# One more weight sum of a feed-forward block made by an adding transfer, its two source blocks loaded in the other order

## The reference

```python
h = rms_norm(x, ffn_norm_g[layer])
x = x + (jax.nn.silu(h @ w_ffn_gate[layer]) * (h @ w_ffn_up[layer])) @ w_ffn_down[layer]
return rms_norm(x, final_norm_g)
```

## Time and profile before

| | |
|---|---|
| median of 3 runs | 381.22 us (380.93 to 381.58) |
| the profiled execution's own time | 381.97 us |
| its span in the trace | 379.8 us |
| TensorE busy | 370.3 us, 97% |
| VectorE busy | 300.0 us, 79% |
| ScalarE busy | 218.1 us, 57% |
| transfers issued by SyncE (q1) | 70.03 MB, 52.9% of 16 engines' span |
| transfers issued by GpSimd (q0) | 3.15 MB, 4.9% of 16 engines' span |
| granted TensorE clock, mean | 0.995 of full |

### The profile page before, as it was taken

One profiled execution on the slowest core, in us unless ns is written; L12 is line 12 of the kernel. 1 busy time (PEld: TensorE's weight loads), 2 busy tenths in 40 slices (PEclk: granted clock), 3 DMA queues, 4 the chain that ended last, 5 costly groups with the idle time before them and its releaser, 6 DMA issues. The chain is left out here.

```text
span 379.8 us, 4716 instructions
## 1 busy us (share of the span) xinstructions
PE 370.3 (97%) x1859; PEld 311.6 (82%) x1859; DVE 300.0 (79%) x354; ACT 218.1 (57%) x253; POOL 39.7 (10%) x40
## 2 busy tenths in 40 slices
PE   7999999999999999999999999999999999999993
PEld 6998888788888888888888888888888888888782
DVE  3899986986366576289768849999999999999625
ACT  4758688675195541445356536864692692687205
POOL 2699020000000040000100000100100100000002
PEclk9999999999999999999999999999999999999998
DMA  7889165947427277166636920795796499361002
GB/s 283 266 267 298 30 200 193 333 138 253 186 62 271 112 286 267 55 221 210 247 98 209 348 107 9 189 360 220 167 344 265 122 300 352 112 220 59 0 2 110
DMA packets 40765, 73.76 MB, mean 194 GB/s; under 512 B 2300, under 2 KB 14632, under 8 KB 40744
## 3 DMA queue, kind: packets, MB, share of 16 engines
q1 hardware_dynamic: 38944, 70.03, 52.9%
q0 software_dynamic: 1584, 3.15, 4.9%
q10 hardware_dynamic: 216, 0.28, 0.2%
HBM read 72.41 MB, written 1.05 MB: 193 GB/s over the span
## 5 line engine op out<-in xcount | busy, mean ns | idle before, releaser
L976 DVE TENSOR_TENSOR w_lo<-w_raw,w_hi 128x2048 fp32r<-128x2048 f32 x33 | 75.0, 2294 | 15.0 <-ACT w_hi L619 15.0
L859 ACT ACTIVATE w_hi<-w_raw 128x2048 fp32r<-128x2048 f32 x33 | 62.8, 1914 | 24.6 <-DVE w_raw L1337 24.6
L619 ACT ACTIVATE w_hi<-w_raw 128x2048 fp32r<-128x2048 f32 x33 | 62.5, 1916 | 22.7 <-DMA w_raw<-in_w_in 10.3
L1357 DVE TENSOR_TENSOR w_lo<-w_raw,w_hi 128x2048 fp32r<-128x2048 f32 x33 | 74.6, 2285 | 0.2 <-ACT w_hi L859 0.2
L1488 PE MATMUL pp<-w_hi,hT 128*128 128x512 f32 x128 | 50.5, 395 | 0.0
L1490 PE MATMUL pp<-w_lo,hT 128*128 128x512 f32 x128 | 49.9, 390 | 0.0
L1489 PE MATMUL pp<-w_hi,hT 128*128 128x512 f32 x128 | 49.8, 389 | 0.0
L1488 PE MATMUL pp<-w_hi,yT_hi 128*128 128x512 f32 (+1 forms) x104 | 40.5, 390 | 0.0
L1490 PE MATMUL pp<-w_lo,yT_hi 128*128 128x512 f32 (+1 forms) x104 | 40.3, 388 | 0.0
L1489 PE MATMUL pp<-w_hi,yT_lo 128*128 128x512 f32 (+1 forms) x104 | 40.2, 387 | 0.0
L1488 PEld LDWEIGHTS pp<-w_hi,hT 128*128 128x128 f32 x128 | 24.0, 188 | 5.5 <-issue 0.7
(11 more groups left out here) (302 smaller groups left out, 696.1 us busy)
## 6 DMA issues: line engine op xcount, KB each, us to landing
w_raw<-in_w_in SPq DMA_DIRECT2D x21, 1024.0 KB, 5.3
w_raw<-in_w_ffn_gate SPq DMA_DIRECT2D x11, 1024.0 KB, 8.5
w_raw<-in_w_ffn_up SPq DMA_DIRECT2D x11, 1024.0 KB, 7.9
w_raw<-in_w_ffn_down SPq DMA_DIRECT2D x11, 1024.0 KB, 8.0
w_raw<-in_w_o SPq DMA_DIRECT2D x4, 1024.0 KB, 5.4
region_b<-in_w_ffn_gate POOLq DMA_DIRECT2D x3, 1024.0 KB, 9.2
w_raw<-in_w_out_attn SPq DMA_DIRECT2D x2, 1024.0 KB, 5.0
w_raw<-in_w_out_mlstm SPq DMA_DIRECT2D x2, 1024.0 KB, 5.0
```

The lines of the kernel that those rows point to most:

```text
L619: nc.scalar.activation(w_hi[:, slot_of(c), :], w_raw[:, c % RAW, :], ACT.Copy).then_inc(hi_ready, 1)
L859: nc.scalar.activation(w_hi[:, slot_of(c), :], form_raw(name, p), ACT.Copy).then_inc(hi_ready, 1)
L976: nc.vector.tensor_tensor(w_lo[:, slot_of(c), :], w_raw[:, c % RAW, :], w_hi[:, slot_of(c), :].bitcast(F32), ALU.subtract).then_inc(lo_rea ...
L1357: nc.vector.tensor_tensor(w_lo[:, slot_of(c), :], form_raw(*FORM[c]), w_hi[:, slot_of(c), :].bitcast(F32), ALU.subtract).then_inc(lo_ready, 1)
```

## The change

The sum T1 of every set leaves VectorE. Block B12 of a set is now loaded ahead of B11. As soon as B12 has landed, GpSimd issues an adding transfer of block B11 from HBM onto the buffer of B12, which makes T1 there. ScalarE's `w_hi` of T1 and VectorE's sum T2 wait for that transfer (`first_grown`). B11 is also loaded as before, for its own product and for T3. GpSimd's loop now runs over all four sets; its wait for B12 of the next set stands behind the T4 transfer of the set before. The raw buffers of the blocks from B12/B11 of set 0 on are dealt out anew by `landings`; the waits that free them keep their counts, position by position.

```diff
 def sum_count(name, p):
-    return 3 * p + SUMS.index(name) + 1
+    return 2 * p + SUMS.index(name)
...
-    return {"T1": ("T1", "T2"), "T2": ("T3",), "B21": ("T4",) if p + 1 == SETS else ()}.get(name, ())
+    return {"T1": ("T2",), "T2": ("T3",), "B21": ("T4",) if p + 1 == SETS else ()}.get(name, ())
...
         if name == "B11":
+            place("B12", p, "T1")
             place("B11", p, "T3")
-            place("B12", p, "T1")
             place("B22", p, "B22")
...
-            for p in range(SETS - 1):
+            for p in range(SETS):
+                pool.wait_ge(chunk_loaded[LANDED["B12", p][0]], LANDED["B12", p][1])
+                src = ffn_source("B11", p)
+                nc.gpsimd.dma_start(as_source(form_raw("T1", p), src), src, accum_op=ALU.add).then_inc(first_grown, 16)
+                if p + 1 == SETS:
+                    continue
                 pool.wait_ge(lo_ready, AT["T2", p] + 1)
                 pool.wait_ge(w_summed, sum_count("T3", p))
...
                 if grown(name, p):
                     act.wait_ge(w_grown, 16 * (p + 1))
+                elif name == "T1":
+                    act.wait_ge(first_grown, 16 * (p + 1))
                 elif name in SUMS:
...
-                if name == "T1":
-                    dve.wait_ge(chunk_loaded[LANDED["B12", p][0]], LANDED["B12", p][1])
-                    nc.vector.tensor_tensor(form_raw(name, p), part, form_raw(name, p), ALU.add).then_inc(w_summed, 1)
-                elif name == "T2":
-                    dve.wait_ge(w_summed, sum_count("T1", p))
+                if name == "T2":
+                    dve.wait_ge(first_grown, 16 * (p + 1))
                     if p:
                         dve.wait_ge(lo_ready, AT["T4", p - 1] + 1)
```

More of the change, by code:

```diff
@@ L424, in build @@
         w_grown = sem("w_grown")
+        first_grown = sem("first_grown")
         part_kept = sem("part_kept")
@@ L1330, in form_sum @@
             def form_sum(name, p):
-                first = {"T1": "B11", "T2": "B22", "T3": "B11", "T4": "B21"}[name]
+                first = {"T2": "B22", "T3": "B11", "T4": "B21"}[name]
                 dve.wait_ge(chunk_loaded[LANDED[first, p][0]], LANDED[first, p][1])
                 part = raw_of(LANDED[first, p][0])
-                if name == "T1":
-                    dve.wait_ge(chunk_loaded[LANDED["B12", p][0]], LANDED["B12", p][1])
-                    nc.vector.tensor_tensor(form_raw(name, p), part, form_raw(name, p), ALU.add).then_inc(w_summed, 1)
-                elif name == "T2":
-                    dve.wait_ge(w_summed, sum_count("T1", p))
+                if name == "T2":
+                    dve.wait_ge(first_grown, 16 * (p + 1))
                     if p:
```

## The result

The changed kernel takes 398.49 us (397.3 to 400.5), the kernel before 381.4 us in the same comparison: a ratio of 1.0454 (95% interval 1.0416 to 1.0492). It is slower by 17 us, where 4 were forecast with a range that ended at 389.2. The profiled execution took 397.3 us with a span of 395.3 us.

The account below looks back on a forecast made before the run. TensorE was taken as the bound, VectorE barely keeping up. With an 11.9 us adding transfer in each set's chain, TensorE would wait 4.2 us at three turns: from the median of 381.22 to 385.4 us, range 380.7 to 389.2.

Parts of the forecast that it names:

- the one late start: TensorE's matmul at 353.23 behind VectorE's join: removing it wins 0.35 us, plus 0.1 us of longer next pitch, 0.45 together.
- The chain and its pieces but a: From one set's T2 start to the next, without the adding transfer's time: 20.9 us (20.6 into set 3).
- S to the issue: From the start of T2 to the issue of the next set's first load by SyncE: 11.73 us.
- I take a = 11.9: Time of T1's adding transfer from GpSimd's start to landing, taken as 11.9 us.
- the high end of 14.5: Longest adding transfer expected: 10.9 us, plus 1.2 for 4 KB packets and 2.4 for q0 being let in late.
- the late entry: q0's adding transfer, issued behind q1's loads, may get its first packets late: 2.4 us in the high estimate.
- the low end: Adding transfer sharing one for one with q1 all the way, 64 packets per us: 10.8 to 10.9 us.
- S1: Start of sum T2 in set 1, forecast at 261.6, where 261.07 is free.
- TensorE has stood at three turns by then, 4.2 us in all: TensorE waits at the turns of sets 1 to 3 for late T2: 0.5, 2.0 and 1.7 us.
- B22 ends within half a us of q0: B22's load on q1 ends about when the adding transfer does; nothing was counted for it.
- The rival of the late entry: GpSimd's queue is held back behind q1, a transfer of 14.5 us, 12 us lost, 393 us; chance 0.06.
- The rival in time: Adding transfer takes at most 10.4 us, TensorE never waits at the turns, 380.8 us; chance 0.33.

## Why the prediction was wrong

The direction was right, and so was the mechanism; the size of one term was not, and the time lay outside the range.

**TensorE is the bound, and relief of VectorE is worth the one late start, 0.45 us together: right as far as the traces show.** The transfer in set 0 alone won nothing. Where VectorE was relieved at its late join, the gap went, and the trace is 0.4 us shorter; the medians there say 0.85. In the changed kernel the late start stayed, as forecast (368.71 after 368.03).

**The chain and its pieces but a: right.** From 264.44 in the changed kernel's trace, and with SyncE's and GpSimd's next issues in set 2,

```profile
276.17 0.37 SPq L514 DMA_DIRECT2D w_raw<-in_w_ffn_up  x1
...
285.14 1.28 POOL L603 DMA_DIRECT2D w_raw<-in_w_ffn_gate  x1 [10.22 <-DMA w_raw<-in_w_ffn_up]
```

S to the issue is 11.73 us as worked out, the landing 8.7, GpSimd's answer 0.3; then 16.7 for the transfer, and 301.91 is the next T2.

**The step that failed: "I take a = 11.9", and the high end of 14.5 with it.** It was 16.0, 16.7 and 15.4 us. Two readings made it small. For the late entry and the bigger packets together I added 1.0 us to the low end, of the 3.6 that I had worked out for both, because the row for the entry showed q1 behind q0 and not the reverse; the entry alone was 2.7 us later than on an idle q1, in each of the sets 1 to 3. And I counted q0 against B11 and B22, 2 KB packets at 64 per us, and the down matrix's 4 KB packets for half of the transfer at most. But the two lengthenings are not independent: while q0 waits to be let in, q1 runs at some 195 packets per us and clears B22, so in sets 1 and 2 all 528 packets then meet dA and dB at 48 per us (in set 3 somewhat under half of them do). In set 1 that is 4.7 us to the first packet, 528 / 48 = 11.0, and 0.3 to land: 16.0. The sum that the prediction set up, with the measured values, gives S1 = 249.6 + 16.0 + 0.1 = 265.7, S2 = 303.3, S3 = 339.3, 16.6 us late, and 397.8 us; 398.5 were measured.

**"TensorE has stood at three turns by then, 4.2 us in all": the place was right, the size follows a.** The turns hold 10.5 us. What I missed is the wait before T1 (2.2 us in all, ScalarE's silu behind its own `w_hi`) and the lower clock after the gaps (1.7 us in set 1 and 1.7 in set 2). With the turns they make 16.1 of the 16.4 us. In sets 1 and 2 these cost nothing of their own, since the next T2 hangs on the chain and not on TensorE: what TensorE loses to them it would have waited at the next turn.

**"B22 ends within half a us of q0": wrong and harmless.** It landed 10 to 12 us earlier.

**The rival of the late entry was nearer than the forecast:** it gave 393 us a chance of 0.06. It was the right mechanism, and its sign held (q0's packets start over 4 us after GpSimd's issue), with a still too short, since it kept half of the transfer on 2 KB packets. The rival in time was wrong: its condition (a at most 10.4) was met in no set of the changed kernel (15.1 us at least); it was met where B22 was held back, and once of three times where dA was.

The Trainium skill ("DMA: Bandwidth & Descriptors", "Queues, rings and completion order") has the DMA engine go round its queues by turns of some 9 to 17 descriptors. The counts agree with equal turns, 145 to 148; how long one turn is they do not show. The delay that I estimated from it, 1.4 us for one turn, does not agree: it was 2.7 us more than on an idle q1, or 2.0 to 2.2 more with only B22 ahead, in the transfers of sets 1 to 3.

## What to carry to other kernels

A sum moved from an engine to an adding transfer becomes a link of the chain that runs through the buffers' reuse; add up that chain from one round to the next before asking how busy the engine is. Size the transfer in the company that it will have: when it is issued, list what the other queue holds and in which packet sizes, because a second queue gets in late and then shares by packets, so big packets beside it make it slow. If it must be done, hold back the loads that nobody needs yet (here that brought the time back to 1 us above the kernel before, not under it); and move work only where the relieved engine is the one waited for.

## What the runs showed of the hardware

- Two queues on the DMA engines share one for one by packets (145 to 148 beside packets of 4 KB, 193 to 195 beside 2 KB). An adding transfer of 2 KB packets moves 98 to 102 per us alone once it is under way, 64 beside 2 KB packets and 48 beside 4 KB packets.
- When q1 holds B22, or B22 and dA, at the issue, q0's first packet comes 4.0 to 4.7 us after GpSimd starts; with only the end of B11 left it comes after 2.0 us, as with q1 idle. Whether q0 stands behind what is already queued, or its own descriptors come slower on a loaded machine, is open; the entry falls on the end of B22's packets in both cases, which speaks for the first (0.1 us behind its last packet in the changed kernel, 0.4 to 0.6 ahead of it where dA is held).
- After gaps of 2.7 to 3.5 us TensorE ran at 1.2 GHz for a while in some places (the 32 starts from the turn's took 8.0 to 9.1 us for 6.3), but after equal gaps elsewhere not at all: the last turn of the changed kernel (gap 3.5 us, 6.4 us), and all turns of the kernel that holds B22 (gaps up to 3.5 us, 6.4 us), whose mean clock was 0.998. In the kernel with 2 KB packets both are seen: gaps of 2.7, 2.5 and 3.5 us at the three turns, then 8.0, 6.4 and 9.0 us. What decides is open. Where a chain sets the pace it costs nothing of its own; where the chain has ended it does, 2.7 us in the two kernels that show it.
